# Down products of two blocks in four as three short-form products, with two gather buffers in place of four

## The chip, the cores and the metric

The kernel runs on one core of a Trainium2 chip. The metric is the device time of one execution in microseconds (us); the median of three runs is quoted. The profile is of one further execution of its own.

## What is computed

One inference step of a one-layer streaming encoder over 576 tokens (512 of a new stream, 64 of a running one) of width 1024. The layer adds to x an attention and recurrence part, then a mixture of experts, and ends with a norm. The change touches only the experts:

```python
def hier_moe(h, ...):          # per token: top-1 group of 4, then top-2 of its 4 experts
    ...
    for e in range(N_EXPERTS):                                   # 16 experts
        y = (silu(h @ w_gate[e]) * (h @ w_up[e])) @ w_down[e]    # 1024 -> 256 -> 1024
        out = out + gates[..., e:e + 1] * y.astype(f32)
```

All inputs are float32. Each token goes to two experts, so there are 1152 token rows over 16 experts, some 72 for each.

## The kernel before, in words

The expert stage is the last large one. Rows of h2 (the normed x) lie in HBM in `h2_dram`. A block is up to 128 rows of one expert; with these inputs there are 16 blocks, one for each expert. `group_of_blocks(i)` handles four of them (`UNROLL` = 4, the slots 0 to 3 of group i); it is written out for group 0 and runs as a loop on each engine for the groups 1 to 3. The engines meet through semaphores alone, and each engine does its own list strictly in order.

For a block, in the order of the work:

- POOL gathers the rows of the block from HBM into the buffer `xg` by an indirect DMA (`gather`, L725 to 728). Before the change `xg` has four buffers (`AHEAD = UNROLL`, L56 and L256), and the gather of block s+4 is issued as soon as block s is turned.
- PE turns the rows (`turn_half`, L2047 to 2051, eight transposes, after a wait on `gathered[...]`, L2093), ACT copies them out as `xT_hi` (L998, the part that a float32r product keeps) and DVE subtracts for the rest, `xT_lo` (L1604).
- The gate and up products: 24 matmuls of 128x512 in float32r (L2089, L2090, L2091: hi by hi, hi by lo, lo by hi, for each of 8 chunks). This three-product form is the short form. The weights are split beforehand in the same way: ACT copies `gu_hi` (L1004, four copies a block), DVE subtracts `gu_lo` in place of the raw weights (L1610, four a block).
- ACT computes silu (L1049), DVE multiplies (L1646), PE turns the 128x256 result `hh` in two transposes (L2101), DVE copies it out as `hhT` (L1652).
- The down product `down` (L2061 to 2071): four matmuls of plain float32 with 512 columns for each block. The trace shows each as two PE instructions, so eight a block (L2069). It waits for `hhT`, for the down weights and for the room of an earlier result.
- ACT and DVE each copy half of the result to `y` (L1042, L1639), and POOL scatters it to HBM (`scatter`, L730 to 734, issued at L748 and L777).

The order on PE within a slot is: gate and up products of block s, turning of block s+1 (this waits for its gather), the down product of block s-1 (slots 1 and 2 only), turning of `hh`, and then the next slot. The down products of the slots 2 and 3 both come at the end of the group (L2103, L2104).

POOL's list in the loop, for slot 0: copy the token numbers (`gather_later`, L752 to 755), gather, copy the next ones, gather, wait for y of slot 0, scatter. For slot 1 and 2: one gather, then wait for y of that slot, then its scatter. For slot 3: wait for y, scatter, with no gather. Gathers and scatters all go through POOL's one DMA queue (q0). The weights go through SP's queue (q1): gate and up of the next group when the gate and up products of their slot are done (L581, L582), down weights when the down product has read them (L584, L585).

The lists of ACT (L1044 to 1055) and DVE (L1641 to 1662) per slot: half of a split ahead for a later block, silu or multiply, `xT`, the other half of the split, `hhT` (DVE), and the result of the slot before (`take_y`). Slot 0 has no split ahead; slot 3 has six weight quarters in place of four.

Of the kernel before, what the change touches and what calls it, by code (L numbers as in the profile page):

```python
# [24 lines left out]
ALU = mybir.AluOpType  # L25
ACT = mybir.ActivationFunctionType
AX = mybir.AxisListType
F32 = mybir.dt.float32
F32R = mybir.dt.float32r
I32 = mybir.dt.int32  # L30

P = 128
D = 1024
KC = D // P
# [18 lines left out]
MAX_OVER = min(MAX_OVER, PAIRS // (P + 1))  # L53
UNROLL = 4
BLOCKS = NE + MAX_OVER
AHEAD = UNROLL  # L56
COLS = (BLOCKS + AHEAD + 1) // 2 * 2
NOWHERE = 4096
TERMS = (TOK - 1) // P
# [34 lines left out]
def program(nc, io):  # L94
    ctx = ExitStack()
    with ctx:
        def sem(name):
            return ctx.enter_context(nc.semaphore(name))

        def sems(name, n):  # L100
            return [sem(f"{name}{i}") for i in range(n)]


        cursor = [(nc.sbuf_base + 63) // 64 * 64]

        def place(name, shape, dt=F32):
            n = int(np.prod(shape[1:])) * 4
            t = nc.alloc_sbuf_tensor_at(name, shape, dt, offset=cursor[0])
            cursor[0] += (n + 31) // 32 * 32
            return t  # L110
# [3 lines left out]
        ident = place("ident", [P, P])  # L114
# [11 lines left out]
        lower_j = place("lower_j", [P, 4, 4])  # L126
        slot_val = place("slot_val", [P, NT, 2, 2])
        g2_bc = place("g2_bc", [P, D])
        ng_bc = place("ng_bc", [P, BW])
        w_route = place("w_route", [P, KC, NG + NE])  # L130
        b_route = place("b_route", [P, NG + NE])
# [13 lines left out]
        table_tok = place("table_tok", [P, COLS], I32)  # L145
        now_tok = place("now_tok", [P, UNROLL, 1], I32)
# [47 lines left out]
        def at(name, shape, dt, offset):  # L194
            return nc.alloc_sbuf_tensor_at(name, shape, dt, offset=offset)
# [43 lines left out]
        def hgrn_buffers(t):  # L239
# [13 lines left out]


        cursor[0] = after_small
        xg = place("xg", [P, UNROLL, D])  # L256
        xT_hi = place("xT_hi", [P, KC, P], F32R)
        xT_lo = place("xT_lo", [P, KC, P], F32R)
        sg = place("sg", [P, FE])
        hh = place("hh", [P, FE])  # L260
        hhT = place("hhT", [P, 2, 2, P])

        gu_hi = [place("gu_hi0", [P, 2, KC, FE], F32R)]
        y = place("y", [P, 2, D])
# [30 lines left out]
        gu_lo = [at(f"gu_lo{i}", [P, 2, KC, FE], F32R, gu_at[i]) for i in range(UNROLL)]  # L295
        we_gu = [at(f"we_gu{i}", [P, 2, KC, FE], F32, gu_at[i]) for i in range(UNROLL)]
        cursor[0] += UNROLL * 2 * KC * FE * 4
        we_d = [place(f"we_d{i}", [P, 2, D]) for i in range(UNROLL)]
        gu_hi.append(place("gu_hi1", [P, 2, KC, FE], F32R))
        assert cursor[0] <= nc.sbuf_usable_end  # L300

# [4 lines left out]
        ps = ctx.enter_context(nc.psum_tensor("ps", [P, 8, 512], F32))  # L306


        h2_dram = nc.dram_tensor("h2_rows", (TOK, D), F32, kind="Internal").ap()
# [42 lines left out]
        expert_in, down_in = sems("expert_in", UNROLL), sems("down_in", UNROLL)  # L352
# [4 lines left out]
        hh_turned, hhT_ready, y_ready, y_act, y_dve = (  # L357
            sem(n) for n in ("hh_turned", "hhT_ready", "y_ready", "y_act", "y_dve"))
        gu_hi_done, gu_lo_done, gates_ready = sem("gu_hi_done"), sem("gu_lo_done"), sem("gates_ready")
        pair_in = [sems(f"pair_in{i}_", NT) for i in range(2)]  # L360
        sum_ready, ssq3_ready, rstd3_ready, final_ready = (
            sem(n) for n in ("sum_ready", "ssq3_ready", "rstd3_ready", "final_ready"))
# [83 lines left out]
        def bank(b, n=512):  # L446
            return ps[:, b, 0:n]
# [160 lines left out]
        def _(pool):  # L608
# [115 lines left out]

            def gather(slot, tokens):  # L725
                pool.indirect_dma_start(
                    xg[:, slot, :], None, h2_dram, bass.IndirectOffsetOnAxis(ap=tokens, axis=0),
                    bounds_check=TOK - 1, oob_is_err=False).then_inc(gathered[slot], 16)

            def scatter(slot, pairs):  # L730
# [6 lines left out]
                gather(s, table_tok[:, s:s + 1])  # L737
            pool.wait_ge(table_ready, 2)
            pool.wait_ge(x_turned_b, 1)
            gather(0, table_tok[:, AHEAD:AHEAD + 1])  # L740
            for s in range(UNROLL):
                following = s + 1 + AHEAD
                if s < UNROLL - 1:
# [13 lines left out]
            with pool.Fori(1, turns) as i:  # L757
                for slot in range(UNROLL):
                    s = UNROLL * i + slot
                    if slot == 0:  # L760
                        gather_later(0, s)
                        pool.wait_ge(col_copied, 2 * s - 2 * UNROLL + 1)
                        pool.sem_inc(dma_cleared, 1)
                        gather(0, now_tok[:, 0, :])
                    if slot < UNROLL - 1:
                        gather_later(slot + 1, s + 1)
                    pool.tensor_copy(now_pair[:, slot, :], table[:, bass.ds(s, 1)]).then_inc(col_copied, 1)
                    if slot < UNROLL - 1:
                        pool.wait_ge(col_copied, 2 * s - 2 * UNROLL + 3)
                        pool.sem_inc(dma_cleared, 1)  # L770
                        gather(slot + 1, now_tok[:, slot + 1, :])
                    else:
                        pool.wait_ge(col_copied, 2 * s - 2 * UNROLL + 2)
                    pool.wait_ge(y_act, s + 3)
                    pool.wait_ge(y_dve, s + 3)
                    pool.sem_inc(dma_cleared, 1)
                    scatter(slot, now_pair[:, slot, :])  # L777
# [6 lines left out]
        def _(act):  # L784
# [253 lines left out]
            def take_y(i, slot):  # L1038
                act.wait_ge(y_ready, UNROLL * i + slot + 1)

                act.wait_ge(stored[slot % 2], 16 * (2 * i + slot // 2 + 1))
                act.activation(y[:, slot % 2, 0:512], bank(4 + 2 * (slot % 2)), ACT.Copy).then_inc(y_act, 1)  # L1042

            def group_of_blocks(i):  # L1044
                for slot in range(UNROLL):
                    s = UNROLL * i + slot
                    split_ahead(slot, i, 0)
                    act.wait_ge(gu_ready, s + 1)
                    act.activation(sg[:, :], ps[:, 0, 0:FE], ACT.Silu).then_inc(silu_ready, 1)  # L1049
                    x_high(s + 1, 0)  # L1050
                    x_high(s + 1, 1)
                    split_ahead(slot, i, 1)
                    if slot:
                        take_y(i, slot - 1)
                take_y(i, UNROLL - 1)

            group_of_blocks(first)
# [13 lines left out]
        def _(dve):  # L1071
# [564 lines left out]
            def take_y(i, slot):  # L1636
                dve.wait_ge(y_ready, UNROLL * i + slot + 1)
                dve.wait_ge(stored[slot % 2], 16 * (2 * i + slot // 2 + 1))
                dve.tensor_copy(y[:, slot % 2, 512:1024], bank(5 + 2 * (slot % 2))).then_inc(y_dve, 1)  # L1639

            def group_of_blocks(i):  # L1641
                for slot in range(UNROLL):
                    s = UNROLL * i + slot
                    split_ahead(slot, i, 0)
                    dve.wait_ge(silu_ready, s + 1)
                    dve.tensor_tensor(hh[:, :], sg[:, :], ps[:, 0, FE:2 * FE], ALU.mult).then_inc(hh_ready, 1)  # L1646
                    x_low(s + 1, 0)
                    x_low(s + 1, 1)
                    if slot < UNROLL - 1:
                        split_ahead(slot, i, 1)  # L1650
                    dve.wait_ge(hh_turned, s + 1)
                    dve.tensor_copy(hhT[:, slot % 2, :, :], ps[:, 3, 0:2 * P].rearrange("p (c t) -> p c t", c=2)  # L1652
                                    ).then_inc(hhT_ready, 1)
                    if i is first and slot in (0, 3):
                        (weights if slot == 0 else steering)()
                    if slot == UNROLL - 1:
                        split_ahead(slot, i, 1)
                    if slot:
                        take_y(i, slot - 1)
                    if i is first and slot == 1:  # L1660
                        over_marks()
                take_y(i, UNROLL - 1)

            group_of_blocks(first)
            over_table()
# [31 lines left out]
        def _(pe):  # L1697
# [349 lines left out]
            def turn_half(slot, half, signal):  # L2047

                for c in range(4 * half, 4 * half + 4):
                    last = pe.transpose(ps[:, 1 + half, (c % 4) * P:(c % 4 + 1) * P], xg[:, slot, c:D:KC], ident[:, :])  # L2050
                last.then_inc(signal, 1)

            def over_slots():
# [7 lines left out]
            def down(i, slot):  # L2061
                pe.wait_ge(hhT_ready, UNROLL * i + slot + 1)

                pe.wait_ge(y_act, UNROLL * i + slot + 1)
                pe.wait_ge(y_dve, UNROLL * i + slot + 1)
                pe.wait_ge(down_in[slot], 16 * (i + 1))
                for half in range(2):
                    for f in range(2):
                        last = pe.matmul(bank(4 + 2 * (slot % 2) + half), hhT[:, slot % 2, f, :],  # L2069
                                         we_d[slot][:, f, 512 * half:512 * half + 512], start=f == 0, stop=f == 1)  # L2070
                last.then_inc(y_ready, 1)
# [78 lines left out]
```

## Time and profile before

| what | us |
|---|---|
| median of three runs | 523.42 |
| lowest and highest | 521.96, 525.18 |
| profiled execution, its own time | 524.19 |
| span of its profile | 522.4 |
| PE busy | 471.7 |
| DVE busy | 336.5 |
| ACT busy | 232.0 |
| POOL busy | 105.7 |

The time of the profiled execution is 1.8 us above its span, and 0.8 us above the median. Rows of the trace count from the span's start. The expert stage runs from about 318.5 to 488.9 us; after it the scattered rows are read back, weighed, normed and stored. In rows of PE the duration of a matmul is its latency; successive ones overlap, and the chain of work shows the step from one to the next.

### The profile page before, as it was taken

The numbers are of one execution on the slowest core, as the hardware profiler recorded it, in microseconds if no ns is written. First come the engines' busy times: TensorE is split into PE (matmuls) and PEld (weight loads), VectorE is DVE, ScalarE is ACT, GpSimd is POOL, SyncE is SP. The second block draws the span as 40 slices with busy tenths as digits, with TensorE's granted clock in tenths as the row PEclk, the third lists the DMA queues.
The fourth block names the chain that finished last, engine by engine and source line by source line (L and its number), as shares of the span: only waits on it lengthen the run. The fifth ranks groups of instructions, "written<-read, shape, count | busy, mean of one in ns | idle before, by whom it ended". The sixth has DMA issues, their size and how long they took to land.

```text
span 522.4 us, 7082 instructions
## 1 busy us (share of the span) xinstructions
PE 471.7 (90%) x2493; PEld 371.8 (71%) x2493; DVE 336.5 (64%) x658; ACT 232.0 (44%) x448; POOL 105.7 (20%) x168
## 2 busy tenths in 40 slices
PE   6999899999999999999999887999999999999400
PEld 6879799877996777778877686676766776677100
DVE  4777515586585357766554689697478567765176
ACT  6664711563356447224121335466367356544021
POOL 5148001111000000001000143030322322312143
PEclk9999999999999999999999959899999999999855
DMA  8804404004008500510110878999899999800295
GB/s 306 194 6 163 169 0 162 0 1 162 1 1 218 163 11 4 178 41 0 41 60 3 304 271 344 421 404 373 333 367 377 375 342 358 338 23 27 69 332 189
DMA packets 33101, 93.16 MB, mean 178 GB/s; under 512 B 10248, under 2 KB 13456, under 8 KB 26928
## 3 DMA queue, kind: packets, MB, share of 16 engines
q1 hardware_dynamic: 27728, 82.81, 44.0%
q0 software_dynamic: 5344, 9.97, 5.4%
q8 instruction: 17, 0.28, 0.2%
q14 instruction: 12, 0.10, 0.1%
HBM read 88.38 MB, written 13.89 MB: 196 GB/s over the span
## 4 chain that ended last, share of the span: by engine, by line
PE 77%; DVE 11%; DMA 5%; ACT 4%; issue 1%; SPq 1%; POOL 0%; POOLq 0%; ACTq 0%; DVEq 0%
PE ps L2069 11%; PE ps L1745 7%; PE ps L1747 7%; PE ps L1746 7%; PE ps L2089 6%; PE ps L2091 5%; PE ps L2090 5%; PE ps L1957 3%; PE ps L1959 3%; PE ps L1958 3%; DMA pair<-y_pairs 2%; PE ps L2050 2%; PE ps L1982 1%; PE ps L1900 1%; PE ps L1897 1%
## 5 line engine op out<-in xcount | busy, mean ns | idle before, releaser
L1610 DVE TENSOR_TENSOR gu_lo<-we_gu,gu_hi 128x1024 fp32r<-128x1024 f32 x64 | 74.8, 1219 | 3.0 <-ACT gu_hi L1004 1.5
L1004 ACT ACTIVATE gu_hi<-we_gu 128x1024 fp32r<-128x1024 f32 x64 | 63.2, 1055 | 3.0 <-DMA we_gu<-in_w_up 3.0
L2069 PE MATMUL ps<-we_d,hhT 128*128 128x512 f32 x128 | 56.9, 592 | 0.0
L2089 PE MATMUL ps<-gu_hi,xT_hi 128*128 128x512 f32 x128 | 52.7, 411 | 2.6 <-DVE xT_lo L1604 2.5
L2091 PE MATMUL ps<-gu_hi,xT_lo 128*128 128x512 f32 x128 | 50.9, 397 | 0.0
L2090 PE MATMUL ps<-gu_lo,xT_hi 128*128 128x512 f32 x128 | 50.5, 395 | 0.0
L1745 PE MATMUL ps<-hT_hi,w_hi 128*128 128x288 f32 x160 | 48.5, 303 | 1.7 <-DVE w_lo_q L1103 0.8
L2069 PEld LDWEIGHTS ps<-we_d,hhT 128*128 128x128 f32 x128 | 23.4, 191 | 24.9 <-issue 24.9
L1745 PE MATMUL ps<-w_hi,hT_hi 128*128 128x512 f32 x96 | 39.1, 407 | 0.0
L1746 PE MATMUL ps<-w_lo,hT_hi 128*128 128x512 f32 x96 | 37.5, 391 | 0.0
L1745 PEld LDWEIGHTS ps<-hT_hi,w_hi 128*128 128x128 f32 x160 | 30.1, 188 | 5.0 <-issue 2.6
L1049 ACT ACTIVATE sg<-ps 128x256 f32<-128x256 f32 x16 | 6.2, 385 | 60.9 <-PE ps L2091 60.9
L1646 DVE TENSOR_TENSOR hh<-sg,ps 128x256 f32<-128x256 f32 x16 | 6.7, 421 | 40.4 <-ACT sg L1049 40.2
L2089 PEld LDWEIGHTS ps<-gu_hi,xT_hi 128*128 128x128 f32 x128 | 24.5, 192 | 8.7 <-issue 2.5
L731 POOL DMA_INDIRECT y_pairs<-y,now_pair x12 | 13.9, 1161 | 79.8 <-DVE y L1639 78.0
L814 ACT ACTIVATE w_hi<-ring,g_col 128x512 fp32r<-128x512 f32 (+1 forms) x48 | 28.7, 680 | 0.0
L1747 PE MATMUL ps<-hT_hi,w_lo 128*128 128x288 f32 x96 | 28.3, 294 | 0.0
L2091 PEld LDWEIGHTS ps<-gu_hi,xT_lo 128*128 128x128 f32 x128 | 24.4, 191 | 5.4
L2090 PEld LDWEIGHTS ps<-gu_lo,xT_hi 128*128 128x128 f32 x128 | 24.4, 191 | 5.3 <-issue 0.5
L1958 PE MATMUL ps<-w_lo,mix_hi 128*128 128x512 f32 x64 | 25.6, 401 | 0.0
L1106 DVE SCALAR_TENSOR_TENSOR w_lo<-ring,g_col,w_hi 128x512 fp32r<-128x512 f32 (+1 forms) x40 | 25.4, 701 | 0.0
L631 POOL TENSOR_SCALAR ms<-osq 128x4 f32<-128x4 f32 (+1 forms) x5 | 1.0, 194 | 115.6 <-ACT logf L916 115.6
(394 smaller groups left out, 1122.3 us busy)
## 6 DMA issues: line engine op xcount, KB each, us to landing
we_gu<-in_w_gate SPq DMA_DIRECT2D x16, 1024.0 KB, 7.7
we_gu<-in_w_up SPq DMA_DIRECT2D x16, 1024.0 KB, 13.0
we_d<-in_w_down SPq DMA_DIRECT2D x16, 1024.0 KB, 12.3
ring<-in_w_in SPq DMA_DIRECT2D x4, 2048.0 KB, 7.7
pair<-y_pairs SPq DMA_DIRECT2D x8, 512.0 KB, 7.7
ring<-in_w_in SPq DMA_DIRECT2D x3, 1024.0 KB, 8.1
x_first<-in_x_p SPq DMA_DIRECT2D x4, 512.0 KB, 9.7
x<-in_x_p SPq DMA_DIRECT2D x4, 512.0 KB, 3.7
```

What stands on the lines that cost most here:

```text
L814: act.activation(w_split(k, w_high(k, c)), w_raw(k, c), ACT.Copy, scale=gain).then_inc(w_hi_done, 1)
L1004: act.activation(gu_hi[slot % 2][:, :, 2 * q:2 * q + 2, :], we_gu[slot][:, :, 2 * q:2 * q + 2, :], ACT.Copy).then_inc(gu_hi_done, 1)
L1106: ins = dve.scalar_tensor_tensor(out, w_raw(k, c), g1_col[:, c:c + 1], hi, ALU.mult, ALU.subtract)
L1610: dve.tensor_tensor(gu_lo[slot][:, :, 2 * q:2 * q + 2, :], we_gu[slot][:, :, 2 * q:2 * q + 2, :], gu_hi[slot % 2][:, :, 2 * q:2 * q + 2, : ...
L1745: pe.matmul(out, stationary[0], moving[0], start=c == 0, stop=False)
L1746: pe.matmul(out, stationary[0], moving[1], start=False, stop=False)
L1747: last = pe.matmul(out, stationary[1], moving[0], start=False, stop=c == KC - 1)
L1958: pe.matmul(out, mix_hi[:, c, 0:r], w_l, start=False, stop=False)
L2069: last = pe.matmul(bank(4 + 2 * (slot % 2) + half), hhT[:, slot % 2, f, :], we_d[slot][:, f, 512 * half:512 * half + 512], start=f == 0, s ...
L2089: pe.matmul(bank(0), xT_hi[:, c, :], gu_h[:, :, c, :], start=c == 0, stop=False)
L2090: pe.matmul(bank(0), xT_hi[:, c, :], gu_l[:, :, c, :], start=False, stop=False)
L2091: last = pe.matmul(bank(0), xT_lo[:, c, :], gu_h[:, :, c, :], start=False, stop=c == KC - 1)
```

## The change

For the slots 0 and 1 of each group (`SHORT = 2`) the down product takes the short form: 12 matmuls in float32r for each block in place of the four of plain float32. For this ACT copies hi parts of the turned `hh` (one copy) and of the down weights (two copies, 128x1024 each), and DVE subtracts for the lo parts, the lo weights in place of the raw ones. The hi weights have one buffer of 8 KB per partition; `xg` goes from four buffers to two (`AHEAD = 2`), so that the gather of block s+2 is issued when block s is turned. The semaphores `gathered` still go by the block's slot. POOL's list keeps its shape; what it gathers at each place is the block two earlier than before.

```diff
-AHEAD = UNROLL
+AHEAD = 2
+SHORT = 2
...
-        xg = place("xg", [P, UNROLL, D])
+        xg = place("xg", [P, AHEAD, D])
+        we_d_hi = place("we_d_hi", [P, 2, D], F32R)
...
+        hhT_at = cursor[0]
         hhT = place("hhT", [P, 2, 2, P])
+        hhT_hi = at("hhT_hi", [P, SHORT, 2, P], F32R, hhT_at)
+        hhT_lo = at("hhT_lo", [P, SHORT, 2, P], F32R, ng_at)
...
+        we_d_lo = [at(f"we_d_lo{i}", [P, 2, D], F32R, d_at[i]) for i in range(SHORT)]
...
-            gather(0, table_tok[:, AHEAD:AHEAD + 1])
+            gather(AHEAD, table_tok[:, AHEAD:AHEAD + 1])
...
-                        gather(0, now_tok[:, 0, :])
+                        gather(AHEAD % UNROLL, now_tok[:, 0, :])
...
-                        gather(slot + 1, now_tok[:, slot + 1, :])
+                        gather((slot + 1 + AHEAD) % UNROLL, now_tok[:, slot + 1, :])
...
+            def hh_high(s, slot):
+                act.wait_ge(hh_turned, s + 1)
+                act.activation(hhT_hi[:, slot, :, :], ps[:, 3, 0:2 * P].rearrange("p (c t) -> p c t", c=2),
+                               ACT.Copy).then_inc(hhT_hi_done, 1)
+
+            def down_high(i, slot):
+
+                act.wait_ge(down_in[slot], 16 * (i + 1))
+                for f in range(2):
+                    act.activation(we_d_hi[:, f, :], we_d[slot][:, f, :], ACT.Copy).then_inc(d_hi_done, 1)
...
                     if slot:
                         take_y(i, slot - 1)
+                    if slot < SHORT:
+                        hh_high(s, slot)
+                        down_high(i, slot)
...
-                    dve.wait_ge(hh_turned, s + 1)
-                    dve.tensor_copy(hhT[:, slot % 2, :, :], ps[:, 3, 0:2 * P].rearrange("p (c t) -> p c t", c=2)
-                                    ).then_inc(hhT_ready, 1)
+                    if slot < SHORT:
+                        dve.wait_ge(hhT_hi_done, SHORT * i + slot + 1)
+                        dve.tensor_tensor(hhT_lo[:, slot, :, :], ps[:, 3, 0:2 * P].rearrange("p (c t) -> p c t", c=2),
+                                          hhT_hi[:, slot, :, :].bitcast(F32), ALU.subtract).then_inc(hhT_ready, 1)
+                    else:
+                        dve.wait_ge(hh_turned, s + 1)
+                        dve.tensor_copy(hhT[:, slot % 2, :, :], ps[:, 3, 0:2 * P].rearrange("p (c t) -> p c t", c=2)
+                                        ).then_inc(hhT_ready, 1)
...
                     if slot:
                         take_y(i, slot - 1)
+                    if slot < SHORT:
+                        down_low(i, slot)
...
+            def down_low(i, slot):
+                for f in range(2):
+                    dve.wait_ge(d_hi_done, 2 * SHORT * i + 2 * slot + f + 1)
+                    dve.tensor_tensor(we_d_lo[slot][:, f, :], we_d[slot][:, f, :], we_d_hi[:, f, :].bitcast(F32),
+                                      ALU.subtract).then_inc(d_lo_done, 1)
...
-                    last = pe.transpose(ps[:, 1 + half, (c % 4) * P:(c % 4 + 1) * P], xg[:, slot, c:D:KC], ident[:, :])
+                    last = pe.transpose(ps[:, 1 + half, (c % 4) * P:(c % 4 + 1) * P], xg[:, slot % AHEAD, c:D:KC], ident[:, :])
...
+                if slot < SHORT:
+                    for f in range(2):
+                        pe.wait_ge(d_lo_done, 2 * SHORT * i + 2 * slot + f + 1)
+                        for half in range(2):
+                            out, cols = bank(4 + 2 * (slot % 2) + half), slice(512 * half, 512 * half + 512)
+                            pe.matmul(out, hhT_hi[:, slot, f, :], we_d_hi[:, f, cols], start=f == 0, stop=False)
+                            pe.matmul(out, hhT_hi[:, slot, f, :], we_d_lo[slot][:, f, cols], start=False, stop=False)
+                            last = pe.matmul(out, hhT_lo[:, slot, f, :], we_d_hi[:, f, cols], start=False, stop=f == 1)
+                    last.then_inc(y_ready, 1)
+                    return
                 pe.wait_ge(down_in[slot], 16 * (i + 1))
```

## Rows read from the trace of the kernel before

**Rows 1.** The page: busy time by engine; chain of the end by engine.

```profile
PE 471.7 (90%) x2493; PEld 371.8 (71%) x2493; DVE 336.5 (64%) x658; ACT 232.0 (44%) x448; POOL 105.7 (20%) x168
...
PE 77%; DVE 11%; DMA 5%; ACT 4%; issue 1%; SPq 1%; POOL 0%; POOLq 0%; ACTq 0%; DVEq 0%
```

**Rows 2.** Windows (us; busy PE, PEld, DVE, ACT, POOL; PEclk; DMA share; GB/s): groups 0, 2, 3.

```profile
318.50:363.10 44.60, 42.74 (x170) 30.15 (x170) 36.32 (x62) 27.59 (x36) 7.08 (x6) 0.96 1.00 402
...
405.60:447.20 41.60, 41.00 (x170) 28.84 (x169) 29.16 (x37) 23.30 (x32) 10.55 (x16) 1.00 0.95 362
447.20:488.80 41.60, 41.00 (x169) 28.58 (x167) 21.95 (x31) 15.85 (x24) 11.28 (x18) 1.00 0.23 93
```

**Rows 3.** The chain of work, group 2 slot 1 to 2: start, us, what.

```profile
418.96 0.88 PE ps L2050 x8
419.83 3.44 PE ps L2069 x8
423.27 0.23 PE ps L2101 x2
423.49 0.23 PE ps L2089
```

**Rows 4.** Costliest groups of the page: the splits of the weights.

```profile
L1610 DVE TENSOR_TENSOR gu_lo<-we_gu,gu_hi 128x1024 fp32r<-128x1024 f32 x64 | 74.8, 1219 | 3.0 <-ACT gu_hi L1004 1.5
L1004 ACT ACTIVATE gu_hi<-we_gu 128x1024 fp32r<-128x1024 f32 x64 | 63.2, 1055 | 3.0 <-DMA we_gu<-in_w_up 3.0
```

**Rows 5.** Timeline of DVE: group 0 slot 2; group 1 slots 1 and 2.

```profile
345.28 0.42 DVE L1646 TENSOR_TENSOR hh<-sg,ps 128x256 f32<-128x256 f32 x1 [0.35 <-ACT sg L1049]
...
377.87 0.42 DVE L1646 TENSOR_TENSOR hh<-sg,ps 128x256 f32<-128x256 f32 x1 [3.12 <-ACT sg L1049]
...
387.90 0.42 DVE L1646 TENSOR_TENSOR hh<-sg,ps 128x256 f32<-128x256 f32 x1 [2.10 <-ACT sg L1049]
```

**Rows 6.** Timeline of POOL from the end of group 1.

```profile
410.61 0.99 POOL L731 DMA_INDIRECT y_pairs<-y,now_pair  x1 [0.91 <-POOL now_pair L767]
...
412.71 1.04 POOL L726 DMA_INDIRECT xg<-h_rows,now_tok  x1 [0.91 <-PE ps L2050]
...
414.94 1.13 POOL L726 DMA_INDIRECT xg<-h_rows,now_tok  x1 [0.88 <-POOL now_pair L767]
...
428.35 1.03 POOL L726 DMA_INDIRECT xg<-h_rows,now_tok  x1 [0.85 <-POOL now_pair L767]
```

**Rows 7.** Line L726 alone in windows of 1 us from 370.5, 412.5, 454 and 428.

```profile
L726 POOL DMA_INDIRECT xg<-h_rows,now_tok x1: 1058/1058/1058, 370.7 to 370.7; - x1
...
DMA to landing us min/median/max: 12.3/12.3/12.3
...
DMA to landing us min/median/max: 11.3/11.3/11.3
...
DMA to landing us min/median/max: 5.0/5.0/5.0
...
DMA to landing us min/median/max: 10.1/10.1/10.1
```

**Rows 8.** The chain: turning after slot 1 in groups 1 and 3; slot 3's end in group 2.

```profile
377.42 0.88 PE ps L2050 x8
...
438.79 0.25 PE ps L2091
...
460.48 0.88 PE ps L2050 x8
```

**Rows 9.** Busy time by window around an idle PE, columns as in rows 2.

```profile
324.00:326.00 2.00, 1.20 (x10) 0.96 (x8) 1.76 (x8) 1.47 (x3) 0.03 (x1) 1.00 1.02 418
326.00:328.00 2.00, 1.07 (x4) 0.84 (x5) 1.81 (x5) 0.00 (x0) 0.96 (x1) 0.95 1.03 430
328.00:330.00 2.00, 2.00 (x6) 1.52 (x6) 1.00 (x7) 1.10 (x2) 0.00 (x0) 0.50 0.97 403
330.00:332.00 2.00, 2.00 (x8) 1.58 (x7) 2.00 (x2) 0.90 (x1) 0.00 (x0) 0.70 1.03 422
```

More of the change, by code:

```diff
@@ L128, in program @@
         g2_bc = place("g2_bc", [P, D])
+        ng_at = cursor[0]
         ng_bc = place("ng_bc", [P, BW])
@@ L297, in program @@
         cursor[0] += UNROLL * 2 * KC * FE * 4
+        d_at = [cursor[0] + i * 2 * D * 4 for i in range(SHORT)]
         we_d = [place(f"we_d{i}", [P, 2, D]) for i in range(UNROLL)]
+        we_d_lo = [at(f"we_d_lo{i}", [P, 2, D], F32R, d_at[i]) for i in range(SHORT)]
         gu_hi.append(place("gu_hi1", [P, 2, KC, FE], F32R))
@@ L359, in program @@
         gu_hi_done, gu_lo_done, gates_ready = sem("gu_hi_done"), sem("gu_lo_done"), sem("gates_ready")
+        d_hi_done, d_lo_done, hhT_hi_done = sem("d_hi_done"), sem("d_lo_done"), sem("hhT_hi_done")
         pair_in = [sems(f"pair_in{i}_", NT) for i in range(2)]
@@ L726, in gather @@
                 pool.indirect_dma_start(
-                    xg[:, slot, :], None, h2_dram, bass.IndirectOffsetOnAxis(ap=tokens, axis=0),
+                    xg[:, slot % AHEAD, :], None, h2_dram, bass.IndirectOffsetOnAxis(ap=tokens, axis=0),
                     bounds_check=TOK - 1, oob_is_err=False).then_inc(gathered[slot], 16)
```

## The prediction

> **What bounds the kernel now.** I read the page first. PE is busy for 471.7 us of the span, and the chain that ends last is 77% PE [rows 1]. So a time matters in so far as it stands on PE's list or makes PE wait. Then the expert stage by windows: the groups 2 and 3 take 41.6 us each, with PE busy for 41.0, DVE for 29 and 22 and ACT for 23 and 16 [rows 2]; group 1 is like group 2. PE is the bound there, but a second resource is close behind it: the DMA share is 1.00 in group 0 at 402 GB/s and 0.95 in group 2 at 362. Only group 3, for which there is no further weight to load, has a share of 0.23. Then the chain in one slot: gate and up products in steps of 0.23 us, turning 0.88 us, the down product 3.44 us, turning of hh 0.23 us, and the next slot without a gap [rows 3]. No wait is in it. Last, POOL's list, since the change alters which block each gather is for.
>
> **PE, the part that is made shorter.** A down product takes 3.44 us for eight instructions [rows 3], 0.43 each. The short form needs 2 x 2 x 3 = 12 matmuls of 128x512 in float32r, of the same shape and types as the gate and up products, whose step is 0.23 [rows 3]: 12 x 0.23 = 2.8 us. That is 0.65 us less for a block. Two blocks in each of four groups make 8 x 0.65 = 5.2 us, all of it on PE's list. The bounds: no less than 0 (if the changed order gained nothing), and no more than 5.2, as the step of these very matmuls is in the trace.
>
> **ACT and DVE, the added splits.** For each of the eight blocks ACT gets two copies of 128x1024 at 1.055 us and one of 128x256, for which I take 0.4; DVE gets two subtractions at 1.22 us [rows 4], while its copy of hhT becomes a subtraction of the same size. That is 2.5 us on ACT and 2.4 us on DVE, for a group 5.0 and 4.9. ACT goes to some 28 us and DVE to some 34 of a group's 40 [rows 2]. What matters is whether they are late somewhere. DVE waits 3.1 us before the multiply of slot 1 [rows 5], which covers the 2.4 us of down_low(0). It waits 2.1 us before that of slot 2 [rows 5], so this one comes about 0.3 us late. That costs nothing, because PE turns x and does the down product for 0.88 + 2.8 us before it needs hh. ACT has wider gaps. In group 0 DVE has more to do (over_marks), and it waits for only 0.35 us before the multiply of slot 2 [rows 5]. There 2.4 us more makes the multiply of slot 2 some 2 to 3 us late, which is 0.3 us more than PE's cover, and it may reach slot 3, where hh is on the path. I take 0.5 us, between 0 (cover as in the other groups) and 2.4 (all of a down_low on the path). PE's wait for the lo parts is met: once ACT has the room they need 2 x 1.055 + 1.22 = 3.3 us, and ahead of the down product PE has the gate and up products of the next slot (24 x 0.23 = 5.5 us) and a turning. If this cover were gone, up to 2.4 us a block would show; that is a rival below.
>
> **The gathers, the part that is made later.** POOL issues at the same places as before, but each place now serves the block two earlier. What counts is the time from a gather's issue to the turning of that block:
>
> - Slot 0's place in the loop (L764) now serves slot 2 of the same group. It comes after both scatters of the group before, since POOL works in order. In group 2 the second scatter starts at 410.61, and the gather at 412.71 [rows 6]. Its block is turned after slot 1, at 418.96 [rows 3]. So it has 6.25 us. That gather took 11.3 us from its start to landing [rows 7], so it landed at 424.0, which is 5.05 us too late. In group 1 the start is 370.7, the landing 12.3 us later at 383.0 [rows 7], the turning at 377.42 [rows 8]: 5.6 us too late. In group 3 the gather is issued at 454.2 and takes 5.0 us as the weights run out [rows 7]; it is due at 460.48 [rows 8], and 1.2 us are left. In group 0 the gather of block 2 is issued before the group begins and has more than 10 us.
> - Slot 1's place now serves slot 0 of the next group. In group 2 it starts at 428.35 and takes 10.1 us [rows 6, 7], so it lands at 438.45. It is due at the end of slot 3's products, at 439.04 [rows 8], and two shorter down products bring that forward by 1.3 us. That is 0.7 us late. Groups 0 and 1 are alike. Between 0 and 0.7 for each of three, I take 0.5 us in sum: behind a stall the weight queue has less on it.
> - The other two places (the gather at 414.94 [rows 6] for slot 3, and slot 2's for the next group's slot 1) have over 14 us against 10 to 12. Nothing.
>
> Both stalls of the first kind are on the path in full. In this time PE has nothing else: turning stands ahead of the down product in its list. ACT and DVE wait too, as `xT` stands ahead of their next splits, so no work is done ahead. What is queued behind PE's wait is the down product of slot 0, the turning of hh and slot 2. SP's next weight loads wait for these. So the sum gets 5.6 + 5.05 = 10.65 us. As the second one comes with a lighter weight queue I take 4.5 for it, and 10.1 for both. The bounds are 0 (a landing below 6 us, as in group 3) and 2 x 6.05 = 12.1 (both at 12.3 us against 6.25).
>
> The Trainium skill has a rule that speaks for less: DMA: Bandwidth & Descriptors, section "Anatomy of one DMA — SWDGE (gpsimd) path", fits 2.0 us plus the bytes over 436 GB/s for a DMA issued from GpSimd. By this estimate a gather of 72 rows of 4 KB takes 2.7 us and no block is late. The trace doesn't agree where weights are being loaded: 12.3, 11.3 and 10.1 us [rows 7]; it comes nearer only in group 3.
>
> **The clock behind a stall.** The granted clock of PE fell once in this stage: PE was busy for only 2.3 of 4 us, and then the clock was 0.50 (the level of 1.2 GHz) for 2 us and 0.70 for 2 more, before it was back at 1.00 [rows 9]. In full-clock terms that is (1 - 0.50) x 2 + (1 - 0.70) x 2 = 1.6 us lost, and 0.1 ahead of it. A stall of 5 us leaves PE idle for longer than that one did. I expect the same fall behind each of the two, 1.7 us each, 3.4 in sum, between 0 and 2 x 2.5 (a low level that lasts half as long again). The Trainium skill, TensorE: Matmul & The Clock Gate, section "HAM oscillation — how this bites in real kernels", says the same of a kernel whose matmuls wait for a DMA again and again: each burst starts at the low clock.
>
> **The sum.** Against the profiled execution's 524.2: -5.2 (down products) + 0.5 (DVE in group 0) + 10.1 (two late gathers) + 0.5 (three slightly late ones) + 3.4 (clock) = +9.3, so 533.5. The profiled execution is 0.8 above the median, so for the median 532.7.
>
> **The rivals.**
>
> - *The gathers land in time.* The weight loads of the moment decide how long a gather takes. If two gathers fewer at the start and a shorter group changed that, or if the landings that I read are not the gathers' own, only the gain is left: 523.4 - 5.2 + 0.5 = 518.7, about 1% faster. For it: 5.0 us in group 3. Against it: 10 us and more in all gathers beside weight loads, also in group 1 where the share is lower. Chance 0.12.
> - *The gathers are late by half of that and the clock holds.* 5 us of stalls against 5.2 of gain: 523.4 - 5.2 + 5 + 1 = 524.2, no change. Chance 0.13.
> - *Stalls as forecast, clock holds.* 532.7 - 3.4 = 529.3. Chance 0.13.
> - *ACT and DVE become the bound.* Slower without any gather late: if the added 2.5 us of a block stood on the path in all eight places, 523.4 - 5.2 + 8 x 2.45 = 537.8. It decides where DVE's wait ahead of the multiply plus PE's cover is under 2.4 us; the wait is 3.1 in slot 1 [rows 5]. On top of late gathers it would be more, 540 and up. Chance 0.07.
> - *The forecast*, both stalls and both falls of the clock, 529 to 538: chance 0.55.
>
> **How the numbers follow.** A change under 1% can't be told from none here: the bounds are 518.2 and 528.7. The case of gathers in time straddles the lower one, so 0.08 for faster. No change takes the rest of that and the half-late case, 0.17. Slower has 0.75. The range reaches down through the half-late case to 520, and up to 539, which is 523.4 - 5.2 + 12.1 + 5.0 + 2.4 + 0.7 = 538.4 and a little.
>
> **What would show it.** In the profile of the changed kernel: 12 matmuls for each of the slots 0 and 1, 96 in all, in steps of 0.23, and 64 of the old kind left. PE idle for some 5 us ahead of the turning behind slot 1 in the groups 1 and 2, put down to the DMA of xg, and none in group 3. A granted clock near 0.5 for 2 to 4 us behind each. Groups 1 and 2 of 45 to 48 us, group 3 of 40.3. The forecast is wrong if the wait for xg is under 3 us in all, if the groups 1 and 2 are under 42 us, or if the idle time ahead of PE is put down to the lo parts of the down weights or of hh.

## The result, and the profile after

The changed kernel takes 531.78 us (median of four runs, 529.13 to 535.6) against 522.69 for the kernel before on the same chips: a ratio of 1.0167, interval 1.0127 to 1.0207. It is slower, as forecast, and the median is 0.9 us from the predicted one. Its runs lie further apart than those of before; why is seen below. The profiled execution is one of the two shortest, 529.59 us with a span of 527.8, against 524.19 with 522.4 before. So the two profiles differ by 5.4 us and the medians by 9.1.

The page of the changed kernel: busy time by engine, and the shares of the chain that ended last by engine and by line (cut from the same page).

```profile
PE 468.4 (89%) x2525; PEld 378.4 (72%) x2525; DVE 351.8 (67%) x674; ACT 249.4 (47%) x472; POOL 109.4 (21%) x166
...
PE 60%; DVE 15%; DMA 13%; issue 4%; ACT 4%; POOL 2%; SPq 1%; POOLq 1%; DVEq 0%; ACTq 0%
DMA xg<-h_rows,now_tok 7%; PE ps L1781 7%; PE ps L1783 7%; PE ps L1782 7%; DVE gu_lo L1633 4%; PE ps L1993 3%; PE ps L1994 3%; PE ps L1995 3%; PE ps L2115 3%; DMA pair<-y_pairs 2%; DMA xg<-h_rows,table_tok 2%; PE ps L2135 2%; PE ps L2018 2%
```

PE is busy for 3.3 us less and the kernel takes longer. The chain was 77% PE [rows 1]; it is 60% now, and 9% of the span is the gather, `DMA xg<-h_rows`, which was nowhere near the top before. The lines moved: L2086 turns x (L2050 before), L2135 to L2137 are the gate and up products, L2107 to L2109 the short down products, L2115 the old ones, L735 the gather and L740 the scatter.

The timeline of PE in the changed kernel, of the expert stage only group 0's first product, the first product of slot 1 in the later groups, and the turnings that had idle time ahead of them (in brackets: idle us, and what ended it):

```profile
316.74 0.50 PE L2135 MATMUL ps<-gu_hi,xT_hi 128*128 128x512 f32 x1 [1.60 <-DVE xT_lo L1627]
...
351.00 1.16 PE L2086 MATMUL ps<-ident,xg 128*128 128x128 f32 x8 [0.74 <-DMA xg<-h_rows,table_tok]
367.77 0.49 PE L2135 MATMUL ps<-gu_hi,xT_hi 128*128 128x512 f32 x1 [0.49 <-DVE xT_lo L1627]
...
377.92 1.97 PE L2086 MATMUL ps<-ident,xg 128*128 128x128 f32 x8 [4.41 <-DMA xg<-h_rows,now_tok]
399.58 0.60 PE L2086 MATMUL ps<-ident,xg 128*128 128x128 f32 x3 [1.05 <-DMA xg<-h_rows,now_tok]
...
415.25 0.49 PE L2135 MATMUL ps<-gu_hi,xT_hi 128*128 128x512 f32 x1 [0.49 <-DVE xT_lo L1627]
...
424.66 1.16 PE L2086 MATMUL ps<-ident,xg 128*128 128x128 f32 x8 [3.68 <-DMA xg<-h_rows,now_tok]
...
445.73 1.16 PE L2086 MATMUL ps<-ident,xg 128*128 128x128 f32 x8 [0.48 <-DMA xg<-h_rows,now_tok]
...
461.42 0.49 PE L2135 MATMUL ps<-gu_hi,xT_hi 128*128 128x512 f32 x1 [0.49 <-DVE xT_lo L1627]
```

These lines are the result. The first products of slot 1 in the groups 1, 2 and 3 start at 367.77, 415.25 and 461.42. The same instruction in the chain of the kernel before:

```profile
371.68 0.49 PE ps L2089
...
413.20 0.49 PE ps L2089
...
454.74 0.49 PE ps L2089
```

Group 0 began at 318.57 before and at 316.74 after. I measure from mark to mark. So the stretch called group 1 below runs from slot 1 of group 1 to slot 1 of group 2, and takes in slot 0 of group 2; group 2 likewise. The stretch of group 0 takes in slot 0 of group 1 as well.

| stretch | before | after | difference |
|---|---|---|---|
| up to group 0 | 318.57 | 316.74 | -1.8 |
| group 0 | 53.1 | 51.0 | -2.1 |
| group 1 | 41.5 | 47.5 | +6.0 |
| group 2 | 41.5 | 46.2 | +4.6 |
| group 3 and the rest | 67.7 | 66.4 | -1.3 |

The sum is +5.4. Group 3 has no wait for xg and shows the gain of two shorter down products, 1.3 us. Groups 1 and 2 each have a long wait behind slot 1 (4.41 and 3.68 us), a short one ahead of the next group's slot 0 (1.05 and 0.48), and something more, since 6.0 + 1.3 is 7.3 and the waits of group 1 make 5.5 (in group 2, 5.9 and 4.2). That rest is the clock. Busy time by window of the changed kernel, around the second long wait (columns as in rows 2):

```profile
422.00:424.00 2.00, 0.00 (x0) 0.00 (x0) 0.00 (x0) 0.00 (x0) 0.00 (x0) 1.00 0.78 295
424.00:426.00 2.00, 1.34 (x10) 1.24 (x11) 0.00 (x0) 0.59 (x2) 0.00 (x0) 0.95 1.01 410
426.00:428.00 2.00, 2.00 (x6) 1.60 (x5) 1.82 (x3) 2.00 (x4) 0.00 (x0) 0.50 1.01 424
428.00:430.00 2.00, 2.00 (x8) 1.57 (x7) 1.83 (x2) 0.38 (x1) 0.00 (x0) 0.70 0.50 209
430.00:432.00 2.00, 2.00 (x11) 1.70 (x10) 0.81 (x2) 1.71 (x4) 0.00 (x0) 1.00 0.39 66
```

All engines stand still from 422 to 424 while the DMA engines are busy; then PE works at 0.50 (1.2 GHz) for 2 us and at a mean of 0.70 for 2 more, the pattern of rows 9. That is 1.7 us in full-clock terms, as in the forecast.

### The profile page after: what moved, and what is told of

It is laid out like the page before. It is cut to its first block, busy times and chain, and to the rows that moved or that the text cites. A ratio compares the mean times of both kernels' runs of the same rounds, so it can differ in the third digit from the quotient of the medians.

```text
span 527.8 us, 7188 instructions
## 1 busy us (share of the span) xinstructions
PE 468.4 (89%) x2525; PEld 378.4 (72%) x2525; DVE 351.8 (67%) x674; ACT 249.4 (47%) x472; POOL 109.4 (21%) x166
## 4 chain that ended last, share of the span: by engine, by line
PE 60%; DVE 15%; DMA 13%; issue 4%; ACT 4%; POOL 2%; SPq 1%; POOLq 1%; DVEq 0%; ACTq 0%
DMA xg<-h_rows,now_tok 7%; PE ps L1781 7%; PE ps L1783 7%; PE ps L1782 7%; DVE gu_lo L1633 4%; PE ps L1993 3%; PE ps L1994 3%; PE ps L1995 3%; PE ps L2115 3%; DMA pair<-y_pairs 2%; DMA xg<-h_rows,table_tok 2%; PE ps L2135 2%; PE ps L2018 2%; PE ps L2137 2%; PE ps L2136 2%
## 5 line engine op out<-in xcount | busy, mean ns | idle before, releaser
L2135 PE MATMUL ps<-gu_hi,xT_hi 128*128 128x512 f32 x128 | 52.1, 407 | 3.3 <-DVE xT_lo L1627 3.1
L2137 PE MATMUL ps<-gu_hi,xT_lo 128*128 128x512 f32 x128 | 50.1, 392 | 0.0
L1627 DVE TENSOR_TENSOR xT_lo<-ps,xT_hi 128x512 fp32r<-128x512 f32 x34 | 22.0, 686 | 14.9 <-ACT xT_hi L1007 14.8
L2135 PEld LDWEIGHTS ps<-gu_hi,xT_hi 128*128 128x128 f32 x128 | 24.1, 188 | 9.3 <-DVE xT_lo L1627 2.3
L740 POOL DMA_INDIRECT y_pairs<-y,now_pair x12 | 12.7, 1060 | 82.5 <-DVE y L1662 80.5
L2086 PE MATMUL ps<-ident,xg 128*128 128x128 f32 x136 | 19.1, 285 | 10.4 <-DMA xg<-h_rows,now_tok 9.6
L2115 PE MATMUL ps<-we_d,hhT 128*128 128x512 f32 x64 | 28.1, 592 | 0.0
L2137 PEld LDWEIGHTS ps<-gu_hi,xT_lo 128*128 128x128 f32 x128 | 24.0, 188 | 5.3
L2086 PEld LDWEIGHTS ps<-ident,xg 128*128 128x128 f32 x136 | 17.8, 192 | 13.4 <-DMA xg<-h_rows,now_tok 11.3
L1007 ACT ACTIVATE xT_hi<-ps 128x512 fp32r<-128x512 f32 x34 | 18.6, 595 | 17.8 <-PE ps L2086 17.2
```

Of the source, the lines that this page charges most:

```text
L2135: pe.matmul(bank(0), xT_hi[:, c, :], gu_h[:, :, c, :], start=c == 0, stop=False)
L2137: last = pe.matmul(bank(0), xT_lo[:, c, :], gu_h[:, :, c, :], start=False, stop=c == KC - 1)
```

## The experiments

**Two buffers alone: e1.** The kernel before with the later gathers, but without the short form and its splits.

```diff
-AHEAD = UNROLL
+AHEAD = 2
-        xg = place("xg", [P, UNROLL, D])
+        xg = place("xg", [P, AHEAD, D])
-                    xg[:, slot, :], None, h2_dram, ...
+                    xg[:, slot % AHEAD, :], None, h2_dram, ...
-            gather(0, table_tok[:, AHEAD:AHEAD + 1])
+            gather(AHEAD, table_tok[:, AHEAD:AHEAD + 1])
-                        gather(0, now_tok[:, 0, :])
+                        gather(AHEAD % UNROLL, now_tok[:, 0, :])
-                        gather(slot + 1, now_tok[:, slot + 1, :])
+                        gather((slot + 1 + AHEAD) % UNROLL, now_tok[:, slot + 1, :])
```

> The kernel before with xg in two buffers and the later gathers, but with its own down products and no added splits. Theory (late gathers and the clock behind them are the loss, the short form is a gain): the waits for xg stay at 4 to 5.5 us behind slot 1 in the groups 1 and 2, the clock falls behind each, and the down products cost 5.2 us more than in the changed kernel; the gather for the next group's slot 0 is just in time, since slot 3 ends later. Time 533 to 537, slower than the changed kernel by 2 to 5. Rival A (the added splits on ACT and DVE are the loss): no loss without them, 521 to 524. Rival B (no late gather without the short form): no wait for xg over 2 us, 521 to 525.

Measured: 535.1 us (531.95 to 536.15), ratio to before 1.0218, interval 1.0177 to 1.0258; by the medians 3.3 us above the changed kernel. The timeline of PE in e1, the instructions with a wait for xg:

```profile
353.19 1.16 PE L2050 MATMUL ps<-ident,xg 128*128 128x128 f32 x8 [0.16 <-DMA xg<-h_rows,table_tok]
...
380.92 1.97 PE L2050 MATMUL ps<-ident,xg 128*128 128x128 f32 x8 [5.22 <-DMA xg<-h_rows,now_tok]
...
428.02 1.97 PE L2050 MATMUL ps<-ident,xg 128*128 128x128 f32 x8 [4.00 <-DMA xg<-h_rows,now_tok]
```

The long waits are there with no split and no short product in the kernel, so both rivals of e1 fall: the loss is that of the two buffers. The short waits of the changed kernel are gone but for 0.16 us, because slot 3 ends later with the old down products.

**The order on POOL: e2 and e7.** Both have two buffers, but each gather stands ahead of the scatter that it followed; the gather for slot 2 stands ahead of both scatters of the group before. Its buffer is free there, since the block two earlier is turned before the down products of the slots 2 and 3. e2 has the rest of the change, e7 has the old down products and no splits.

```diff
             def gather_later(slot, s):
-                pool.wait_ge(x_turned_b, s + 1)
-                pool.tensor_copy(now_tok[:, slot, :], table_tok[:, bass.ds(s + AHEAD, 1)]).then_inc(col_copied, 1)
+                pool.wait_ge(x_turned_b, s + 2)
+                pool.tensor_copy(now_tok[:, slot, :], table_tok[:, bass.ds(s + 1 + AHEAD, 1)]).then_inc(col_copied, 1)
...
-                        gather(AHEAD % UNROLL, now_tok[:, 0, :])
+                        gather((1 + AHEAD) % UNROLL, now_tok[:, 0, :])
...
-                        gather((slot + 1 + AHEAD) % UNROLL, now_tok[:, slot + 1, :])
+                        gather((slot + 2 + AHEAD) % UNROLL, now_tok[:, slot + 1, :])
```

Group 0, which is written out, is shifted in the same way, and the tables have two columns more than in the changed kernel.

> The changed kernel with each gather issued ahead of the scatter that stood before it in POOL's list (the gather for slot 2 ahead of both scatters of the group before). Buffers, splits and products are the same. Theory: no wait for xg is left, the clock doesn't fall in the groups 1 to 3, each of them takes 40.3 us, time 514 to 518. Rival A (splits are the loss): groups of 42 us and more, time as the changed kernel or 1 to 2 less. Rival C (gathers are slow because the two buffers bring them into the weight loads): landings of 10 us as before, but that doesn't matter any more; what would matter is scatters that come later, by 1 to 2 us, and make y wait: 518 to 522.

> The kernel before with two buffers and each gather issued ahead of its scatter, and the old down products without added splits. Theory: no wait for xg; what is left of the change is the shorter memset, so 520.5 to 521.5. Against e2 it gives the worth of the short form by itself: 5.2 us if ACT and DVE have the room that I worked out, less than 4 if the splits show.

Measured: e2 516.67 us (516.11 to 518.34), ratio 0.9883, interval 0.985 to 0.9916. e7 522.18 us (518.76 to 523.68), ratio 0.9975, interval 0.9951 to 1.0. So e2 came as expected; the median of e7 is 0.7 us above its expected range, and e7 can't be told from the kernel before. The waits of PE in the expert stage of e2, longest first in total:

```profile
PE ps L2137 <- DVE xT_lo L1629: 2.9, 4, 1.4
PE ps L2149 <- DVE hh L1671: 1.4, 1, 1.4
```

No wait for xg is left between its groups; the landing of its gathers in the loop is as slow as ever (11.4 and 8.8 us for the first two of group 1), but now there is time for it. The windows of its four groups:

```profile
316.70:360.90 44.20, 42.50 (x192) 32.64 (x193) 42.66 (x67) 32.09 (x43) 6.84 (x7) 1.00 1.01 410
361.10:401.30 40.20, 39.60 (x178) 30.28 (x177) 33.75 (x44) 27.66 (x38) 9.56 (x15) 1.00 0.94 370
401.30:441.50 40.20, 39.60 (x178) 30.27 (x177) 33.33 (x41) 27.66 (x38) 9.73 (x16) 1.00 0.94 374
441.50:481.70 40.20, 38.34 (x171) 28.92 (x169) 25.62 (x34) 20.20 (x30) 10.77 (x18) 1.00 0.27 108
```

Against rows 2 a group lasts 40.2 in place of 41.6 us, with DVE busy for 33.3 in place of 29.2 and ACT for 27.7 in place of 23.3: the splits are in full view and cost nothing. The first products of slot 1 in the groups 1, 2 and 3, from the chains of e2 and then of e7:

```profile
367.21 0.49 PE ps L2137
407.43 0.49 PE ps L2137
447.65 0.49 PE ps L2137
```

```profile
367.04 0.49 PE ps L2091
408.56 0.49 PE ps L2091
450.10 0.49 PE ps L2091
```

From mark to mark e2 takes 40.22 us in the groups 1 and 2 and e7 takes 41.52 and 41.54: 1.3 us for two blocks, 0.65 each. In group 0 it is 50.50 against 51.34, only 0.84. This is the place where DVE has over_marks to do, and 0.5 us of the gain is lost. Over the whole kernel the short form is worth 5.5 us by the medians of e2 and e7. (The two profiled executions differ by 3.1 only: that of e7 is one of its shortest, reached the expert stage 1.0 us earlier and was 0.7 us quicker behind it.)

By the medians e2 is faster than the changed kernel by 15 us, and than the kernel before by 1.2%.

**The clearing of xg: e3.** In the changed kernel the clearing is made as long as before; it covers the room of the hi weights too, which nothing uses yet.

```diff
+        hi_at = cursor[0]
         we_d_hi = place("we_d_hi", [P, 2, D], F32R)
+        cleared = at("cleared", [P, 2 * AHEAD, D], F32, hi_at - AHEAD * D * 4)
...
-            pool.memset(xg[:, :, :], 0.0).then_inc(xg_clear, 1)
+            pool.memset(cleared[:, :, :], 0.0).then_inc(xg_clear, 1)
```

> The changed kernel, in which POOL clears 16 KB per partition (as before) in place of 8. Theory of a side gain: the memset of xg took 3.5 us before and blocked a TENSOR_SCALAR of DVE for 1.89 us (0.18 after), ahead of the routing chain; so the expert stage starts 1.6 to 1.8 us earlier with two buffers. Then this kernel is slower than the changed one by 1.5 to 1.8 us, and the TENSOR_SCALAR takes some 1.9 us again. Rival: the earlier start came from the clock or from chance: no difference over 0.5 us.

Measured: 532.0 us (531.03 to 533.94), ratio 1.0171. By the medians that is no difference from the changed kernel (531.78), whose runs are too far apart to show 1.5 us. The traces decide it. POOL and DVE in e3, then in the changed kernel (timelines):

```profile
299.26 3.50 POOL L724 MEMSET cleared<- 128x4096 f32 x1
...
300.90 1.89 DVE L1404 TENSOR_SCALAR rt<-rt 128x4 f32<-128x4 f32 x1
```

```profile
298.96 1.80 POOL L722 MEMSET xg<- 128x2048 f32 x1
...
300.61 0.18 DVE L1402 TENSOR_SCALAR rt<-rt 128x4 f32<-128x4 f32 x1
```

In both the TENSOR_SCALAR comes at the same place. With the long memset it ends just as that one does (302.8), with the short one it takes 0.18 us. Counted from the start of the last group of router products in the trace (301.21 in e3, 301.00 in the changed kernel) the expert stage starts after 16.96 us in e3 (318.17) and after 15.74 in the changed kernel. With the long memset of the kernel before it is 16.92; with the short one it is 15.73 in e1, 15.60 in e2 and 15.73 in e7. So 1.2 us of the 1.8 that the changed kernel is earlier are the shorter memset, less than the 1.5 to 1.8 expected. The rest was there before those products and isn't the change's.

**The clock: e4.** Ahead of PE's wait for slot 2's gather in the groups 1 to 3 stand 28 matmuls into a bank that is free at that point.

```diff
+                    if slot == 1 and i is not first:
+                        pe.wait_ge(y_act, UNROLL * i + 2)
+                        pe.wait_ge(y_dve, UNROLL * i + 2)
+                        for _ in range(28):
+                            pe.matmul(ps[:, 7, 0:2 * P], decay_m[:, 0, :], decay_m[:, :, :], start=True, stop=True)
                     pe.wait_ge(gathered[following], 16 * (i + (slot + 1) // UNROLL + 1))
```

> The changed kernel with 28 dummy matmuls of 128x256 (some 3.3 us) on PE ahead of its wait for the gather of slot 2, in the groups 1 to 3. They shorten no wait, they only keep PE active in it. Theory (the low clock behind a wait is a cost of its own, 1.7 us each): the groups 1 and 2 get 1.5 to 2 us shorter each and show no granted clock under 0.9 behind the wait; group 3, which has no wait, gets 3.3 us longer; in sum -3.5 + 3.3, no change within 1.5 us. Rival: the clock costs nothing beyond the wait: groups 1 and 2 as long as before, time 2 to 4 us longer.

The changed kernel was run once more beside it:

> The changed kernel once more, on the chip of the next two, as their measure: 529 to 534, with waits for xg of 3.5 to 4.5 us behind slot 1 in the groups 1 and 2.

Measured: e4 533.8 us (529.94 to 535.69), the changed kernel 533.27 (527.24 to 536.09; 532.19 without the slowest run). The waits of the changed kernel, 6.02 and 3.23 us, are both outside the 3.5 to 4.5 expected. The totals agree with the theory, but the spread doesn't exclude the rival. Nor do whole groups: the stretch of group 1 is no shorter in e4 (47.5 us, as in the first profile of the changed kernel), because its gather took 12.7 us to land. The traces decide behind the wait. PE's turnings in e4, and the windows behind them:

```profile
380.54 1.16 PE L2086 MATMUL ps<-ident,xg 128*128 128x128 f32 x8 [3.06 <-DMA xg<-h_rows,now_tok]
...
425.23 1.16 PE L2086 MATMUL ps<-ident,xg 128*128 128x128 f32 x8 [0.27 <-DMA xg<-h_rows,now_tok]
```

```profile
380.00:382.00 2.00, 1.46 (x10) 1.38 (x11) 0.08 (x1) 0.71 (x2) 0.00 (x0) 1.00 0.88 360
382.00:384.00 2.00, 2.00 (x10) 1.65 (x9) 1.86 (x3) 2.00 (x3) 0.00 (x0) 1.00 0.41 170
...
426.00:428.00 2.00, 2.00 (x12) 1.70 (x11) 1.29 (x2) 2.00 (x4) 0.00 (x0) 1.00 1.05 434
```

I count from the turning behind the long wait to the first product of slot 1 in the next group, less the short wait in between, so that the length of the long wait is out. The kernel of e3 is the changed one but for its clearing, so its groups stand beside the others:

| kernel, group | long wait | lowest granted clock behind it | rest of the stretch |
|---|---|---|---|
| changed, 1 | 4.41 | 0.50 | 36.3 |
| changed, 2 | 3.68 | 0.50 | 36.3 |
| e3, 1 | 3.83 | 0.50 | 37.1 |
| e3, 2 | 3.46 | 0.50 | 36.0 |
| e0, 1 | 6.02 | 0.50 | 36.1 |
| e0, 2 | 3.23 | 1.00 | 34.7 |
| e4, 1 | filled, then 3.06 | 1.00 | 34.7 |
| e4, 2 | filled, then 0.27 | 1.00 | 34.7 |

For example, changed, 1: 415.25 - 377.92 - 1.05 = 36.28. Among these a group with a fall of the clock takes 1.3 to 1.6 us more for the same work, and 2.4 in e3's group 1, where the clock stood at 0.50 for the whole of the windows from 380 to 386. In e0's group 2 it didn't fall, and the rest is as short as in e4. The windows of e0 behind its second wait, for comparison with those above:

```profile
422.00:424.00 2.00, 0.18 (x1) 0.19 (x2) 0.00 (x0) 0.00 (x0) 0.00 (x0) 1.00 0.92 303
424.00:426.00 2.00, 2.00 (x14) 1.77 (x14) 0.80 (x2) 1.43 (x3) 0.00 (x0) 1.00 0.94 391
426.00:428.00 2.00, 2.00 (x11) 1.72 (x10) 1.85 (x3) 1.67 (x3) 0.00 (x0) 1.00 1.03 434
```

**The traffic beside the gather: e5.** SP's loads of 2 MB for the next group's slot 0 wait for the turning of slot 2's block, and those for slot 1, which come next in SP's list, wait with them. POOL's list is that of the changed kernel.

```diff
-                    sp.wait_ge(gu_ready, UNROLL * (i - 1) + slot + 1)
+                    if slot == 0:
+                        sp.wait_ge(x_turned_a, UNROLL * (i - 1) + 3)
+                    else:
+                        sp.wait_ge(gu_ready, UNROLL * (i - 1) + slot + 1)
                     expert(slot, UNROLL * i + slot, 0, 2)
```

> The changed kernel in which SP's loads of gate and up weights for slot 0 of the next group (2 MB) wait until the block of slot 2 is turned, so that the late gather runs beside less traffic. Nothing changes in POOL's order. Theory (the gather is slow because it shares the DMA engines with the weight loads): its landing falls from 10 or 11 us to 6 to 8, the two waits for xg behind slot 1 to under 1.5 us each; time 519 to 524, unless the weights held back come too late, which would show as a wait of ACT for we_gu. Rival (it is slow because two scatters are ahead of it in POOL's queue): landing over 9 us and waits over 3 us as before, time 529 or more.

Measured: 522.77 us (519.74 to 527.08), ratio 0.9982, interval 0.9958 to 1.0007; 10.5 us faster than the changed kernel beside it (9.4 without the slowest run of that one), with the same order of gathers and scatters. Line L738 (the gather) of e5 alone, in windows that hold the one for slot 2 in group 1 and in group 2:

```profile
L738 POOL DMA_INDIRECT xg<-h_rows,now_tok x1: 1062/1062/1062, 367.5 to 367.5; - x1
...
DMA to landing us min/median/max: 8.2/8.2/8.2
...
L738 POOL DMA_INDIRECT xg<-h_rows,now_tok x1: 1046/1046/1046, 412.9 to 412.9; - x1
...
DMA to landing us min/median/max: 5.4/5.4/5.4
```

In the changed kernel they took 10.7 and 9.5 us, and 12.3 and 9.0 in e0. So the weight loads make the gather slower by 2.5 to 4.1 us, and the rival (only the scatters ahead of it) falls. They don't account for all of it: in group 1 of e5 the weight queue q1 moved only 0.26 MB from 368 to 374, and the landing was still 8.2 us, with two scatters and a second gather on POOL's queue. How much of that is the scatters' is not shown apart. Two details I had wrong. The wait in group 1 is 1.94 us, not under 1.5: the down weights of the slots 2 and 3, which e5 doesn't hold, were still loading at its start. And a wait shows in group 3, where the changed kernel has none; PE's timeline in e5:

```profile
463.40 1.16 PE L2089 MATMUL ps<-ident,xg 128*128 128x128 f32 x8 [3.54 <-DMA xg<-h_rows,now_tok]
```

The held loads end later and are still under way when the last group's gather is issued (454.03; it landed 9.3 us later). That profile is of the slowest run of e5 (527.08 us) and is no shorter than that of e0, which is of the fastest run there (527.24). So the 10 us stand on the medians of twelve and six runs, and in the profiles only the waits of the groups 1 and 2 show them. Whether the other runs of e5 have the wait in group 3 is open.

Not tried: the short form with four buffers of xg, for which this layout has no room beside the tables of the overflow blocks.

## Why the prediction was right

- **The short form's gain, forecast 5.2 us:** e2 against e7 has 5.5 by the medians, and by groups 0.84 + 1.30 + 1.32 + 1.31 = 4.8 in the two traces (the last up to DVE's last copy of y, at 480.49 and 484.25). The step of the short matmuls is that of the gate and up products, as taken.
- **The splits, forecast hidden but for 0.5 us in group 0:** shown by e2 and e7, 0.46 lost in group 0 and nothing in the others.
- **The late gathers of slot 2, forecast 5.6 and 4.5 us and none in group 3:** 4.41 and 3.68 in the first profile, 6.02 and 3.23 in e0, 3.83 and 3.46 in e3, 5.22 and 4.00 in e1, none in group 3. The cause is that of the forecast: two buffers (e1), behind two scatters (e2), beside the weight loads (e5). In the first profile the room was 6.4 and 5.8 us (forecast 6.7 and 6.25), and the landings were 10.7 and 9.5 in place of 12.3 and 11.3, so the term was some 2 us too large there. The second wait is the shorter one each time, by 0.4 to 2.8 us; the forecast had 1.1.
- **No wait in group 3, forecast from a landing of 5.0 us:** this row was misread. The 5.0 us of [rows 7] are not those of a gather that moves rows. With four buffers the gathers issued in group 3 are for the blocks 16 to 19, and only 16 blocks hold tokens. The pages show it: POOL's queue q0 (packets, MB, share of the DMA engines) moves as many bytes in both kernels, though the kernel before issues 20 gathers and the changed one 18. Before, then after:

```profile
q0 software_dynamic: 5344, 9.97, 5.4%
...
q0 software_dynamic: 5056, 9.97, 5.1%
```

  In the changed kernel the gather at that place is for block 14, and it landed in 4.1 us. So the forecast of no wait there came true by luck as far as that row goes; that the weights run out by then was its sound half.
- **The slightly late gathers for slot 0, forecast 0.5 in sum:** 0.74, 1.05 and 0.48, so 2.3. This term was mis-sized. The rows gave between 0 and 0.7 for each, so up to 2.1 for the three, and I counted on shorter landings behind a stall; the upper end of the range, 538.4, has the 0.7 only once. In group 0 POOL's instruction itself took longer: the gather issued at 339.36 took 2.24 us in place of 1.47 before (at 343.23 there). It started 0.16 us behind DVE's `over_slot` of over_marks (128x1280, 339.20 to 340.68); the subtractions of the down weights had ended at 339.29. Before, over_marks was done when the gather started. All five profiles with the changed kernel's order on POOL and with the splits have the 2.24, and e1, with the same order and no splits, has 1.42. So the splits bring it about, by moving over_marks onto the gather; that DVE holds POOL up there is argued from the traces, not tested.
- **The clock, forecast 1.7 us behind each stall:** 1.3 to 1.8 where it fell (e1 counted against e7), and once 2.4 (e3, group 1). It fell behind three of the four long waits in the two profiles of the changed kernel, behind both of e1, both of e3 and both of e5, and not behind e0's second one.
- **What the forecast didn't have:** the shorter memset, -1.2 us, and a clock that stays up in group 0. Before, the clock fell at 328 [rows 9]; in the changed kernel it didn't. The windows of the changed kernel for that stretch:

```profile
324.00:328.00 4.00, 3.08 (x13) 2.46 (x14) 3.72 (x11) 2.67 (x5) 0.99 (x1) 1.00 1.01 426
328.00:332.00 4.00, 4.00 (x24) 3.45 (x23) 3.99 (x5) 2.27 (x4) 0.00 (x0) 1.00 1.01 412
```

This is worth some 1.7 us of group 0's -2.1. The fall is in the profiles of the two kernels with the long memset (before and e3) and in none of the seven profiles with the short one. That goes together, but why is open.

The profiled execution is 529.6 where the forecast had 533.5. The two terms left out make -2.9 us of that, shorter stalls than assumed (8.1 in place of 10.1) -2.0, the clock some -0.4, and the short waits for slot 0 give 1.8 back: -3.5 of -3.9. The median agrees better, since other runs are slower by up to 6 us. That it agrees to 0.9 us is luck: terms that were left out and terms that were too large cancel against a spread that the forecast did not have. The long waits differ from run to run in the profiles (3.2 to 6.0 us), and the loss with them; a wait that ends with a DMA landing brings its spread into the time. e2, without such waits, has runs within 2.2 us.

## What to carry to other kernels

When a buffer ring is made shorter, do for each place in the issuing engine's list what was done here: from its row the time of issue, the time of use of the block that it now serves, and the landing time under the load of that moment. A landing of 11 us with four buffers is hidden and shows in no list of waits; the same one with two is the new bound. And see that the row read is of the same work: a gather for an empty block moves no rows, and in the timeline it looks like any other.

Before giving up on the ring's length, look at what stands ahead of the gather on its engine. Here a scatter stood there for no need, and taking the gather first was worth 15 us, three times the gain for which the buffers were given up.

## What was not expected of the hardware

- A memset of POOL holds up a TENSOR_SCALAR of DVE on other data: 1.89 us in place of 0.18, ending with the memset; doubling the memset in e3 brings it back. DVE's TENSOR_TENSOR and TENSOR_REDUCE ran beside the memset before at their usual 0.24 us. The Trainium skill, SBUF — State Buffer, section "SBUF: two separate sides", says that a DVE instruction in a mode with two ports and a GpSimd instruction lock the shared pair of ports against each other for the whole instruction. The trace agrees as to what was held and what was not; whether this TENSOR_SCALAR ran in such a mode, no run shows.
- Whether PE's clock falls behind a wait doesn't go by the wait's length alone: it fell behind 1.94 us (e5, group 1) and not behind 3.23 us (e0, group 2). Nor did it behind the 3.06 us of e4's group 1, ahead of which the dummy matmuls had kept PE busy for 3.5 us.
